# Sums one tick sooner, one gather more in flight, and ScalarE's ticks earlier, in an encoder trunk on one core

## The chip, the cores and the metric

The kernel runs on one core of one Trainium2 chip. The metric is the device time of one execution in microseconds (us). TensorE (PE in the profile), VectorE (DVE), ScalarE (ACT) and GpSimd (POOL) run programs of their own, in order, and wait for one another through semaphores; SyncE (SP) only issues DMA. All DMA queues share the 16 DMA engines of the core.

## What is computed

Two sequences of 256 tokens with 1024 channels go through the same two layers. A layer is

```
x += W_out(sig(gA) * P_A(SSD(n)) + sig(gB) * P_B(DilatedAttn(n))),  n = RMSNorm(x)
x += PEER(RMSNorm(x))
```

SSD is a bidirectional state-space branch in 8 groups, the attention has 24 heads with three dilations, and a last RMSNorm closes the trunk. PEER is the part that the change touches. For each token, 8 heads search two sets of 128 keys, keep the best 16 pairs each, and so choose 128 of 16384 experts. Then

```
hid = gelu(einsum('td,thkd->thk', xb, expert_u[ib]))
out = einsum('thk,thkd->td', gb * hid, expert_v[ib])
```

Each token reads 128 rows of 2048 floats (the u and v halves side by side), all chosen by its own data.

## The kernel before, in words

**Passes.** The work is cut in four passes m (`PASSES`): layer 0 of sequence 0, layer 0 of sequence 1, then layer 1 of each. A pass has a mixer (norm, 8 SSD groups, 4 attention head pairs, 8 merge steps, the output projection, a second norm, 16 query projections, and the routing that yields expert indices and gates) and a PEER part of 256 slots (`SLOTS_P`): two tiles of 128 tokens with 128 slots each. A slot is one expert per token, 128 rows of 8 KB, gathered by one indirect DMA. The PEER part of pass p runs beside the mixer of pass p+1, except its first slots in pass 0 and all 256 of the last pass, which run alone at the end: the tail.

**A slot in steps.** In slot n (k inside its pass):

- POOL gathers the rows into buffer n % NB of eight (`gather`, L559), after the sum of slot n-8 has freed it (`summed`, L461).
- VectorE takes the dot of the u halves with the normed token, into `hid` (L1451).
- ScalarE, once per pair of slots, waits for both dots, computes the gelu (L1041) and two weights (L1046), and for a slot whose sum is on PE a diagonal matrix with the weight (L1054).
- The sum adds weight times v half to the output: on VectorE into x (L1460), or on PE with the diagonal into a PSUM bank (L851). Tables in the code (`BESIDE`, `ON_PE`) say which; in most of the SSD phase odd slots go to PE and even ones to VectorE, in attention and merge nearly all go to VectorE, in the tail all go to PE.

**Ticks.** Each engine has one `tick(p, k)` per slot. VectorE's does the dot of k and then the sum of k - LAG; PE's does the sum of k - LAG (`sums_after`, L155). The last tick of a pass does LAG + 1 sums, and the tick k = 128 + LAG also adds the PE sums of the first tile to x (L1462). ScalarE's acts on odd k. POOL's issues the gather of n + AHEAD, where `AHEAD = NB - LAG - 1`. So 8 buffers hold 4 gathers on their way, one dot, and 3 that wait for their sum.

**The order on each engine** is written out by a planner. `EACH` gives a nominal length in units (about a microsecond each) to every phase, `place(name, i, f)` turns a point in a phase into a position, and the mixers on all engines yield positions between pieces of work. `deal` gives each slot a due position (L105). `together` (L228) runs the ticks due before the next yielded position. ScalarE alone passes a third argument, `BEHIND`: its ticks come that many units later against its mixer work than on the other engines. In the SSD phase a due position comes every 3.6 units, and a group has 42.5.

**Mixer work around the ticks,** as the prediction names it: in SSD group g ScalarE computes 12 decay exponentials twice (L915, for group g-1; the second time just ahead of the second convolution), evacuates four projections with the convolution's middle tap (L943), on which VectorE adds four taps (L1262), then does Silu (L951, L955) and evacuates two small products (L960, L962). VectorE masks the decay rows (L1276), which POOL writes to DRAM (L526) and reads back broadcast (L520) on the queue of the gathers. In the query phase ScalarE evacuates queries (L1024) and key scores (L1018) for VectorE's search (L1096). The projections on PE are L592, with weights loaded by SP into a ring of six units (L488).

Of the kernel before, what the change touches and what calls it, by code (L numbers as in the profile page):

```python
# [66 lines left out]


NB = 8
LAG = 3  # L70
AHEAD = NB - LAG - 1
DIAGS = 5

BEHIND = 3.0


REST = PIECES - PH
# [77 lines left out]
def sums_after(k):  # L155

    return list(range(SLOTS_P - LAG - 1, SLOTS_P)) if k == SLOTS_P - 1 else [k - LAG] if k >= LAG else []

# [69 lines left out]
def together(mixer, tick, late=0.0):  # L228

    for m in range(PASSES):  # L230
        todo = list(PLAN[m])
        for where in mixer(m):
            while todo and todo[0][2] + late <= where:
                tick(*todo.pop(0)[:2])
        while todo:
            tick(*todo.pop(0)[:2])


def build(nc, x_prompt, x_sample, consts, biases, rel, par, w_ssd, w_att, w_mrg, w_out, w_qry, w_uv,
          w_n2, w_final, y_prompt, y_sample):  # L240
    with ExitStack() as ctx:
# [620 lines left out]
        def _(act):  # L862
# [204 lines left out]

            together(mixer, tick, BEHIND)
            for k in range(SLOTS_P):
# [9 lines left out]
        def _(v):  # L1079
# [354 lines left out]
            def add_sums(p, t):  # L1434

                k = SLOTS_T * (t + 1) - 1
                v.wait_ge(v_pe, pe_sums(p, k))
                if dve_sums(p, k):
                    v.wait_ge(v_dve, dve_sums(p, k))
                xo = x[:, 2 * (p % 2) + t, :]  # L1440
                v.tensor_tensor(xo, xo, sum_banks(p, t).rearrange("p b d -> p (b d)"), ALU.add).then_inc(x_add.sem, 1)

            def tick(p, k):
# [8 lines left out]
                for q in sums_after(k):  # L1452
# [5 lines left out]
                    if dve_sums(p, q) > 1:  # L1458
                        v.wait_ge(v_dve, dve_sums(p, q) - 1)
                    v.scalar_tensor_tensor(out=xo, in0=rows[before % NB][:, D:], scalar=wgt[:, q:q + 1], in1=xo,  # L1460
                                           op0=ALU.mult, op1=ALU.add).then_inc(v_dve, 1)
                if k == SLOTS_T + LAG:  # L1462
                    add_sums(p, 0)
# [104 lines left out]
```

## Time and profile before

| | us |
|---|---|
| median of 3 runs | 4060.14 |
| lowest, highest | 4059.96, 4065.61 |
| the profiled execution's own time | 4058.57 |
| span of its profile | 4056.8 |
| PE busy in the span | 3436.7 |
| VectorE busy | 2872.2 |
| ScalarE busy | 1612.8 |
| POOL busy | 1218.2 |
| read from memory | 1439.31 MB |

The profile's page gives busy time by engine, the chain that ended last, groups of instructions, and DMA issues. Busy shares are means over phases with different limits, so the stretches have to be read one by one. In a row of waits the first name is the engine and tile that waited, and the one behind the arrow is what released it. Line numbers are those of the kernel.

### The profile page before, as it was taken

What the parts mean: (1) busy time and instruction counts of PE and PEld (TensorE: products, weight loads), DVE (VectorE), ACT (ScalarE), POOL (GpSimd) and SP (SyncE); (2) the same over time, 40 slices, a digit from 0 to 9 for tenths busy, and PEclk for the clock granted to TensorE, in tenths of its full rate; (3) what the DMA queues carried; (4) which work ended last, traced back from release to release, by engine and by line L of the source; (5) the groups of instructions that cost most, each with busy time, mean ns of one, the idle gap of its engine ahead of it and who ended that gap; (6) DMA issues with size and microseconds to landing.
All of it is one profiled execution on the core that took longest, in us unless ns stands there. A gap on an engine that the chain in (4) does not pass through costs nothing.

```text
span 4056.8 us, 40644 instructions
## 1 busy us (share of the span) xinstructions
PE 3436.7 (85%) x13410; PEld 2350.3 (58%) x13410; DVE 2872.2 (71%) x5740; ACT 1612.8 (40%) x4211; POOL 1218.2 (30%) x1094
## 2 busy tenths in 40 slices
PE   7999997989889787888889787988889886777776
PEld 6877875656667564566667564666667562332222
DVE  3632128898887779899787779899788778655444
ACT  4643013566434223676434223576434222222222
POOL 1000002333333224333333224333333224433332
PEclk9999998989999988999999998999999988999999
DMA  6543447999999988999999989999999979999998
GB/s 205 174 160 127 149 138 293 391 364 396 399 421 423 423 315 353 377 398 412 405 425 420 423 311 355 378 395 415 402 425 419 423 278 365 427 427 427 427 427 351
DMA packets 252119, 1444.49 MB, mean 356 GB/s; under 512 B 31608, under 2 KB 31608, under 8 KB 118788
## 3 DMA queue, kind: packets, MB, share of 16 engines
q0 software_dynamic: 164976, 1133.94, 68.6%
q1 hardware_dynamic: 86800, 307.82, 20.4%
q8 instruction: 107, 1.75, 0.2%
q14 instruction: 104, 0.85, 0.1%
q10 hardware_dynamic: 132, 0.12, 0.0%
HBM read 1439.31 MB, written 7.13 MB: 357 GB/s over the span
## 4 chain that ended last, share of the span: by engine, by line
DMA 30%; PE 28%; DVE 24%; ACT 11%; issue 6%; POOL 1%; DVEq 0%; ACTq 0%; POOLq 0%
DMA rows<-in_w_uv,idx 28%; PE banks L592 16%; DVE rows L1451 7%; DVE x L1460 5%; PE sums L851 4%; ACT arena L915 4%; DVE arena L1262 3%; PE banks L851 2%; PE banks L728 1%; ACT L1041 1%; ACT L915 1%; DMA arena<-a_rows 1%; DVE arena L1288 1%; DVE arena L1359 1%; ACT diag L1054 1%
## 5 line engine op out<-in xcount | busy, mean ns | idle before, releaser
L559 POOL DMA_INDIRECT rows<-in_w_uv,idx x1024 | 1170.8, 1143 | 2209.9 <-DVE x L1460 1309.2
L1451 DVE CUSTOM_DVE_ANT_0 rows<-rows,xn 128x1024 f32<-128x1024 f32 x1024 | 1242.3, 1221 | 521.5 <-DMA rows<-in_w_uv,idx 519.3
L592 PE MATMUL banks<-hT,ring 128*128 128x256 f32 x6656 | 1496.2, 382 | 39.7 <-ACT arena L960 17.3
L592 PEld LDWEIGHTS banks<-hT,ring 128*128 128x128 f32 x6656 | 1267.0, 191 | 293.3 <-issue 92.5
L851 PE MATMUL sums<-rows,diag 128*128 128x512 f32 x1648 | 835.3, 644 | 265.8 <-ACT diag L1054 239.7
L851 PEld LDWEIGHTS sums<-rows,diag 128*128 128x128 f32 x1648 | 322.2, 204 | 656.3 <-ACT diag L1054 325.5
L1041 ACT ACTIVATE gelu<-hid 128x2 f32<-128x2 f32 x512 | 103.7, 203 | 1450.9 <-DVE hid L1451 1449.7
L1460 DVE SCALAR_TENSOR_TENSOR x<-rows,wgt,x 128x1024 f32<-128x1024 f32 x484 | 620.3, 1282 | 31.0 <-ACT wgt L1046 30.0
L1262 DVE SCALAR_TENSOR_TENSOR arena<-banks,pr,arena 128x254 f32<-128x254 f32 (+1 forms) x512 | 245.9, 481 | 119.1 <-ACT arena L943 105.3
L851 PE MATMUL banks<-rows,diag 128*128 128x512 f32 x512 | 239.7, 612 | 76.0 <-ACT diag L1054 76.0
L1046 ACT ACTIVATE wgt<-gelu,gate 128x1 f32<-128x1 f32 x1024 | 246.0, 287 | 16.8
L915 ACT ACTIVATE arena<-arena 128x128 f32<-128x128 f32 x768 | 230.8, 388 | 20.2 <-DVE arena L1276 19.6
L592 PE MATMUL banks<-yT,ring 128*128 128x256 f32 x1024 | 228.4, 380 | 0.7 <-DMA ring<-in_w_mrg 0.6
L851 PEld LDWEIGHTS banks<-rows,diag 128*128 128x128 f32 x512 | 93.3, 192 | 222.4 <-ACT diag L1054 127.9
L592 PEld LDWEIGHTS banks<-yT,ring 128*128 128x128 f32 x1024 | 193.3, 190 | 33.5 <-issue 5.1
L1054 ACT ACTIVATE diag<-cst,wgt 128x128 f32<-128x128 f32 x540 | 193.8, 390 | 4.5
L1041 ACT ACT_TABLE_LOAD x142 | 182.2, 1283 | 2.5
L728 PE MATMUL banks<-ring,hT 128*128 128x384 f32 x512 | 173.3, 492 | 0.0
L1359 DVE CUSTOM_DVE_ANT_1 arena<-banks,arena 128x768 f32<-128x768 f32 x64 | 60.9, 951 | 129.6 <-PE banks L716 129.6
L728 PEld LDWEIGHTS banks<-ring,hT 128*128 128x128 f32 x512 | 95.3, 190 | 71.2 <-issue 12.0
L807 PE MATMUL banks<-ring,arena 128*128 128x512 f32 x256 | 111.8, 595 | 4.8 <-DMA ring<-in_w_out 4.8
L975 ACT ACTIVATE arena<-banks 128x256 f32<-128x256 f32 x96 | 35.9, 380 | 188.5 <-PE banks L592 188.3
(204 smaller groups left out, 2527.9 us busy)
## 6 DMA issues: line engine op xcount, KB each, us to landing
ring<-in_w_ssd SPq DMA_DIRECT2D x192, 512.0 KB, 7.4
ring<-in_w_att SPq DMA_DIRECT2D x144, 512.0 KB, 7.8
ring<-in_w_mrg SPq DMA_DIRECT2D x128, 512.0 KB, 12.4
arena<-a_rows POOLq DMA_DIRECT2D x32, 1024.0 KB, 11.3
ring<-in_w_qry SPq DMA_DIRECT2D x64, 512.0 KB, 5.0
arena<-bias_tiles POOLq DMA_DIRECT2D x16, 1152.0 KB, 9.7
ring<-in_w_out SPq DMA_DIRECT2D x32, 512.0 KB, 17.9
rows<-in_w_uv,idx POOLq DMA_INDIRECT x1024, 12.5
```

What stands on the lines that cost most here:

```text
L559: nc.gpsimd.indirect_dma_start(out=rows[n % NB][:, :], out_offset=None, in_=w_uv, in_offset=bass.IndirectOffsetOnAxis(ap=idx[:, t, s:s + 1 ...
L592: mm = pe.matmul(out, w[:, k * P:(k + 1) * P], rhs[:, k0 + k, :], start=start and k == 0, stop=stop and k == n - 1)
L728: mm = pe.matmul(pb(t, 3 * P), hT[:, k, t * P:(t + 1) * P], w[:, k * 3 * P:(k + 1) * 3 * P], start=(k == 0), stop=(k == KD - 1))
L807: mm = pe.matmul(pb(2 + 2 * t + nh), mT[:, k, t * P:(t + 1) * P], ring_of(u)[:, nh * 512:(nh + 1) * 512], start=k == 0, stop=k == KD - 1)
L851: mm = pe.matmul(sum_banks(p, t)[:, h, :], diag[e % DIAGS][:, :], rows[n % NB][:, D + 512 * h:D + 512 * h + 512], start=q == mine[0], stop ...
L915: ins = act.activation(Eb[:, r, k, :], Eb[:, r, k, :] if src is None else src, ACT.Exp, bias=bneg[:, si, col:col + 1])
L1041: act.activation(gelu[:, k - 1:k + 1], hid[:, k - 1:k + 1], ACT.Gelu).then_inc(g_ge, 1)
L1046: act.activation(wgt[:, q:q + 1], gelu[:, q:q + 1], ACT.Copy, scale=gate[:, t, q % SLOTS_T:q % SLOTS_T + 1]).then_inc(g_w, 1)
L1054: act.activation(diag[e % DIAGS][:, :], ident, ACT.Copy, scale=wgt[:, q:q + 1]).then_inc(d_ok, 1)
L1262: ins = v.scalar_tensor_tensor(out=acc, in0=pb(j)[:, lo + o:lo + o + w], scalar=pr[:, col:col + 1], in1=acc, op0=ALU.mult, op1=ALU.add)
L1451: v.tensor_tensor_reduce(u, u, xn2[:, (n // SLOTS_T) % 3, :], 1.0, 0.0, ALU.mult, ALU.add, hid[:, k:k + 1]).then_inc(u_done, 1)
L1460: v.scalar_tensor_tensor(out=xo, in0=rows[before % NB][:, D:], scalar=wgt[:, q:q + 1], in1=xo, op0=ALU.mult, op1=ALU.add).then_inc(v_dve, 1)
```

## The change

`LAG` goes from 3 to 2, and with it `AHEAD` from 4 to 5; `BEHIND` goes from 3.0 to 1.0. The eight buffers then hold 5 gathers on their way, one dot and 2 that wait for their sum.

```
 NB = 8
-LAG = 3
+LAG = 2
 AHEAD = NB - LAG - 1
 DIAGS = 5
 
-BEHIND = 3.0
+BEHIND = 1.0
```

## Rows read from the trace of the kernel before

**Rows 1.** Stretches: PE, PEld, DVE, ACT, POOL busy (instructions), PE clock, DMA share, GB/s

```profile
740.00:1100.00 360.00, 320.09 (x1303) 227.78 (x1302) 311.79 (x511) 223.33 (x560) 124.24 (x105) 0.95 0.97 388
...
1425.00:1575.00 150.00, 117.34 (x436) 78.84 (x434) 127.34 (x452) 35.05 (x113) 48.65 (x38) 0.89 0.85 319
...
1640.00:2010.00 370.00, 327.75 (x1347) 231.71 (x1346) 323.33 (x528) 229.42 (x576) 132.18 (x113) 0.97 0.98 398
2010.00:2350.00 340.00, 278.74 (x1181) 207.66 (x1180) 268.09 (x384) 116.22 (x277) 115.01 (x102) 0.94 1.01 423
...
3410.00:4056.80 646.80, 485.44 (x1024) 190.01 (x1024) 343.07 (x618) 174.01 (x656) 250.66 (x249) 0.97 0.98 415
```

**Rows 2.** Gathers in 100 us of the tail: POOL busy (gathers), PE clock, DMA share, GB/s

```profile
3500.00:3600.00 100.00, 40.78 (x41) 0.97 1.01 427
```

**Rows 3.** Waits of DVE, 2010 to 2350 and then 3410 to 4056.8: total, times, longest

```profile
DVE rows L1451 <- DMA rows<-in_w_uv,idx: 64.8, 59, 2.5
...
DVE rows L1451 <- DMA rows<-in_w_uv,idx: 288.9, 238, 3.0
```

**Rows 4.** Waits of DVE, 1640 to 2010 (three), then 740 to 1100, 2560 to 2900

```profile
DVE arena L1262 <- ACT arena L943: 15.3, 7, 3.3
DVE rows L1451 <- DMA rows<-in_w_uv,idx: 11.4, 10, 1.7
DVE x L1460 <- ACT wgt L1046: 9.9, 3, 4.5
...
DVE rows L1451 <- DMA rows<-in_w_uv,idx: 5.5, 5, 2.3
...
DVE rows L1451 <- DMA rows<-in_w_uv,idx: 4.0, 4, 2.3
```

**Rows 5.** Waits over the whole span

```profile
ACT gelu L1041 <- DVE hid L1451: 1449.7, 365, 12.9
...
PE sums L851 <- ACT diag L1054: 239.7, 122, 12.9
...
DVE x L1460 <- ACT wgt L1046: 30.0, 10, 4.5
```

**Rows 6.** Groups of the page: busy, mean ns of one, idle before, releaser

```profile
L1460 DVE SCALAR_TENSOR_TENSOR x<-rows,wgt,x 128x1024 f32<-128x1024 f32 x484 | 620.3, 1282 | 31.0 <-ACT wgt L1046 30.0
...
L1046 ACT ACTIVATE wgt<-gelu,gate 128x1 f32<-128x1 f32 x1024 | 246.0, 287 | 16.8
...
L1054 ACT ACTIVATE diag<-cst,wgt 128x128 f32<-128x128 f32 x540 | 193.8, 390 | 4.5
```

**Rows 7.** Timeline, 1774 to 1783: start, us, engine, line, operation, idle before

```profile
1774.65 0.20 ACT L1041 ACTIVATE gelu<-hid 128x2 f32<-128x2 f32 x1
...
1775.71 0.55 ACT L943 ACTIVATE arena<-banks,pr 128x256 f32<-128x256 f32 x1
1776.27 1.28 ACT L915 ACT_TABLE_LOAD   x1
...
1776.29 2.04 DVE L1262 SCALAR_TENSOR_TENSOR arena<-banks,pr,arena 128x254 f32<-128x254 f32 x4 [3.21 <-ACT arena L943]
1777.57 3.62 ACT L915 ACTIVATE arena<-arena 128x128 f32<-128x128 f32 x12
...
1781.73 2.03 DVE L1262 SCALAR_TENSOR_TENSOR arena<-banks,pr,arena 128x254 f32<-128x254 f32 x4
1782.95 0.20 ACT L1041 ACTIVATE gelu<-hid 128x2 f32<-128x2 f32 x1
```

**Rows 8.** Timeline of POOL and then DVE, first SSD group of the pass

```profile
1625.51 0.74 POOL L520 DMA_DIRECT2D arena<-a_rows  x1 [1.31 <-DMA a_rows<-arena]
...
1637.46 2.36 DVE L1276 TENSOR_TENSOR arena<-arena,cst 128x1024 f32<-128x1024 f32 x2 [5.63 <-DMA arena<-a_rows]
```

**Rows 9.** DMA issues of the page: queue, count, KB each, median us to landing

```profile
ring<-in_w_ssd SPq DMA_DIRECT2D x192, 512.0 KB, 7.4
...
arena<-a_rows POOLq DMA_DIRECT2D x32, 1024.0 KB, 11.3
```

**Rows 10.** Timeline of ACT in the query phase

```profile
1490.82 0.38 ACT L1024 ACTIVATE yT<-banks 128x256 f32<-128x256 f32 x1 [2.86 <-PE banks L592]
...
1493.93 0.20 ACT L1041 ACTIVATE gelu<-hid 128x2 f32<-128x2 f32 x1 [2.73 <-DVE hid L1451]
```

## The prediction

> **What bounds the kernel now.** I read the table of stretches first, cut where the phases of a pass change. A pass has three kinds of stretch [rows 1]. In attention and merge (2010 to 2350 us; 1100 to 1425 and 2900 to 3260 read alike) the DMA engines are full, share 1.01 and 423 GB/s, and no other engine is. In the SSD phase (740 to 1100, 1640 to 2010, and 2560 to 2900 alike) the DMA share is 0.97 to 0.98 and VectorE is busy for 323 of 370 us; the queries and the routing (1425 to 1575, twice more after that) leave the DMA at 0.85 with VectorE at 127 of 150 us. The last stretch, 3410 us to the end, is gathers alone at full rate, 41 in 100 us [rows 2]: 2.44 us per gather.
>
> Then the waits of VectorE. Where the DMA is full it waits for gathered rows, 64.8 us in one such stretch and 288.9 us in the last one [rows 3]. In an SSD stretch it waits for ScalarE instead: 15.3 us for a convolution's first tap (L943), 9.9 us for a weight (L1046); rows cost it 11.4 us there, 5.5 and 4.0 us in the two sister stretches [rows 4]. Over the kernel the weight costs VectorE 30.0 us, while ScalarE itself sits 1449.7 us waiting for dots and PE 239.7 us waiting for diagonals [rows 5]. So DMA rate sets some 1670 us, VectorE with ScalarE in its chain most of the rest after the first gather.
>
> **The change, part by part.** AHEAD is NB - LAG - 1, so LAG of 2 alone makes it 5. The gather of slot n+5 stands at POOL's tick n and waits for the sum of n-3, which VectorE or PE now does at tick n-1. The relation of POOL to the sums is the old one; a buffer is given back one tick sooner. No instruction is added or removed, and the order of the sums stays. Moved by one tick are each sum on VectorE and on PE, the addition of a tile's PE sums to x after its first half, and, at the end of a pass, one sum out of the flush (three in place of four), which was on PE and leaves VectorE's flush of three as it is: 0.
>
> *1. Full stretches and the tail.* A fifth gather does not move bytes faster where the share is 1.01 [rows 1]. In the tail POOL, PE and ScalarE have nothing but ticks, each waits for its own slot, and LAG orders nothing: 0. What counts is how far the gathers are ahead when a full stretch begins: VectorE waits for rows all through it [rows 3], so one gather more already in a buffer is one gather less to wait for. That is 2.44 us [rows 2] in each of three passes: -7.3 us. Bounds 0 and -7.3.
>
> *2. Waits for rows in the SSD stretches,* 5.5 + 11.4 + 4.0 = 20.9 us [rows 4], each shorter than one tick. A buffer given back a tick sooner can end any of them, but VectorE may then reach the next wait for ScalarE sooner. Bounds 0 and -20.9; I take a bit over half, -12.
>
> *3. The sum's wait for its weight.* A sum takes 1282 ns, one weight 287 ns and a diagonal 390 ns [rows 6]. An even slot's pair is complete one dot before its sum instead of two; ScalarE needs 0.2 us for the gelu and 0.3 us for the weight, and 1.28 us more for a table if it comes from Exp. With BEHIND 1.0 ScalarE's tick stands two units earlier in its program. Comparing the positions, I find that about 40 of the 128 double ticks of a pass move ahead of a neighbouring item, 17 of them in the SSD phase, and that no table load is added. Three of these move ahead of the decay exponentials (12 ACTIVATEs, 3.62 us). There the weight is early, but the exponentials are late. One case worked out [rows 7]: now the gelu of slots 52 and 53 is at 1774.65, the convolution that VectorE needs is ready at 1776.26, the exponentials start at 1777.57 and the next gelu follows at 1782.95. After the change the sum of slot 52 (1.28 us) goes into VectorE's 3.21 us wait: -1.2. But the tick of slots 54 and 55 moves ahead of the exponentials and holds them until its dot at about 1779.6; 1.1 us of tick, 1.28 of table, 3.62 and 0.55 bring the second L943 to 1786.1, where VectorE starts that convolution at 1781.73 now. In between it can do the sum of slot 54, so +4.4 - 1.3 = +3.1. Nothing moves for the ticks of slots 41 and 67, but their sums come one dot sooner and wait for the same exponentials: some +1.2 and +1.9 by the same working. The two longest weight waits of now (slots 28 and 98) only become waits for exponentials, -0.7 together, and slot 104 adds some 0.9. Net an estimate of +5.4 per pass, +16 in three. Bounds: -30.0, all weight waits gone and nothing in their place [rows 5], and +43: the 15.3 us of L943 [rows 4] nearly doubled in each pass.
>
> *4. POOL's own transfers.* Decay rows go on the queue that the gathers use. In the first SSD group VectorE waits for them: issued at 1625.51, used at 1637.46 after 5.63 us of idle time [rows 8]. They land after 11.3 us where a weight unit on SP's queue takes 7.4 us [rows 9]. One gather more ahead of them is up to 2.44 us [rows 2], unless it fell into idle DMA time before: bounds 0 and +7.3 over three passes, I take +4.5. The Trainium skill, page "DMA: Bandwidth & Descriptors", section "Queues, rings and completion order", says that each DMA engine takes turns between the queue rows that have work, a packet at a time; by that rule the weight loads lose nothing to the fifth gather and the decay rows, in the gathers' row, pay all of it. The sum would then be 3 us higher. The two landing times agree with the rule in direction only.
>
> *5. Queries.* The tick of slot 231 moves ahead of a query evacuation: now the evacuation is at 1490.82 and the gelu at 1493.93 [rows 10]. It holds the evacuation 4.2 us; the key scores that need it are a unit away, so of this about 1 us reaches VectorE: +3 in three passes, bounds 0 and +12.6.
>
> *6. PE.* A sum on PE stands one tick sooner and waits longer for its diagonal. PE runs ahead of VectorE in the SSD phase, so I charge 0: the cover is that lead. If it goes, each pass pays up to 10 us (PE is busy for 328 of 370 us, rows 1, and 35 us more of waits would leave nothing): 0 to +30. The moved ticks also hold Silu of two groups by some 5 us; PE then evacuates its first projection at least 4 us ahead of need, 0.
>
> Sum: -7.3 - 12 + 16 + 4.5 + 3 = +4.2 us on the profiled execution's 4058.57, so 4062.8; that execution is 1.6 us under the median of three, 4060.14. I say 4063. About 0.2%, 8 us, is what a measurement of this kernel can tell from no change.
>
> **Rivals.**
> *A. The early release wins, faster.* If VectorE rarely stands behind the exponentials, item 3 gives back its 30.0 us instead of costing 16, item 2 all 20.9, item 1 its 7.3: 4058.6 - 58 = 4000 at the far end. Half of that, 4030, is likelier, as the L943 waits stay. For it: the long waits of rows 5 are all ScalarE finishing late, and BEHIND of 1.0 goes at that. Against it: what follows those weights is the same ScalarE program. Chance 0.31.
> *B. ScalarE in order holds the mixer, slower.* Place: conv evacuations, exponentials and Silu that stand behind a tick whose dot is late. Each moved item waits for a dot that VectorE does only after its own mixer work. Price: +43 instead of +16 in item 3, and 12.6 in item 5: about +41 on the forecast's terms, 4100. It decides once the waits for L943 pass some 25 us per SSD stretch. For it: ScalarE already idles 1449.7 us for dots. Against it: VectorE's use of a convolution is three units behind ScalarE's place, so much of a delay is covered. Chance, with a smaller version at 4075: 0.25.
> *C. PE loses its lead.* Item 6 at 30: 4092. It decides where the diagonal waits of PE in an SSD stretch grow past the 40 us it has idle. Chance 0.09.
> **How the numbers follow.** Forecast case (terms cancel, 4052 to 4072) 0.35, A 0.31, B 0.25, C 0.09. The forecast case lies within 8 us of the median for nearly all its weight; a little of it, 0.02, is slower. So faster 0.31, same 0.33, slower 0.36. The forecast's own range is 4048 to 4078; for 8 in 10 it reaches to the middle of A, 4032, and into B and C, 4094.
>
> **What would show it.** In the changed profile: the span of the last stretch (first tail dot to the end) unchanged within 2 us; DMA share in the full stretches still 1.01; the wait for rows in SSD stretches under 10 us in all; the gelu soon after its dot before exponentials, but more wait for L943 or for the sums' weights, some 30 us per pass together against 25 now; the wait for decay rows 1 to 2.5 us longer per pass; PE's diagonal waits up without L592 work arriving late. If the weight waits fall to near nothing and L943 stays at 15 us, A is right; if L943 or the decay exponentials rise past 25 us per stretch, B is. A tail that changes, or full stretches that lose share, would prove the reading of the bound wrong.

## The result and the profile after

The changed kernel is slower: 4110.46 us (median of 4 runs, 4106.84 to 4114.64) against 4060.05 us before on the same chip, a ratio of 1.0123 with a 95% interval of 1.011 to 1.0136. The forecast was 4063 us with a range up to 4094 us. The span of its profile is 4112.8 us against 4056.8; the profiled execution, 4114.64 us, is the slowest of the four.

The first view is the table of stretches of the kernel after, cut at the same events of VectorE in each pass: first convolution of the SSD phase, first scores of attention, first addition of the output projection, first dot of the next pass. Columns as in [rows 1]. The first row is pass 1's SSD phase, the second its stretch with full DMA (attention to output); then come pass 2's norm, SSD phase, full stretch and queries, and last the tail.

```profile
710.00:1079.00 369.00, 325.05 (x1279) 227.23 (x1278) 307.07 (x534) 220.24 (x551) 122.92 (x106) 0.94 0.95 370
1079.00:1431.00 352.00, 318.48 (x1380) 235.60 (x1379) 274.54 (x401) 126.92 (x300) 121.73 (x105) 0.97 1.01 418
...
1587.00:1624.00 37.00, 22.12 (x80) 14.40 (x81) 24.62 (x46) 17.36 (x37) 9.78 (x9) 0.73 0.85 330
1624.00:2001.00 377.00, 330.31 (x1288) 230.08 (x1287) 314.22 (x544) 222.24 (x558) 128.99 (x110) 0.93 0.97 374
2001.00:2370.00 369.00, 325.36 (x1380) 241.02 (x1378) 289.24 (x420) 128.96 (x309) 130.12 (x111) 0.95 1.01 416
2370.00:2526.00 156.00, 117.60 (x436) 78.42 (x436) 134.94 (x462) 40.03 (x121) 49.20 (x41) 0.87 0.86 331
...
3464.00:4112.80 648.80, 479.94 (x1024) 187.68 (x1024) 344.65 (x621) 174.00 (x656) 249.80 (x252) 0.98 0.98 415
```

The kernel before, cut at the same events, has this for pass 2 and the tail:

```profile
1575.00:1605.00 30.00, 21.85 (x95) 16.43 (x96) 23.33 (x45) 16.47 (x33) 9.08 (x9) 0.83 0.95 376
1605.00:1960.00 355.00, 315.74 (x1273) 222.26 (x1272) 313.39 (x545) 222.57 (x561) 127.42 (x110) 0.97 0.98 396
1960.00:2332.00 372.00, 319.65 (x1379) 237.05 (x1377) 289.66 (x420) 129.81 (x309) 127.17 (x112) 0.96 1.01 419
2332.00:2490.00 158.00, 116.77 (x436) 78.81 (x436) 135.44 (x463) 40.18 (x120) 52.24 (x41) 0.90 0.84 319
...
3408.00:4056.80 648.80, 485.44 (x1024) 190.01 (x1024) 344.57 (x620) 174.01 (x656) 252.10 (x251) 0.97 0.98 415
```

VectorE is busy for the same time in the SSD phase, 313 and 314 us, but the phase takes 377 us and not 355. With the starts of these events to a tenth, over all passes:

| us | before | after | difference |
|---|---|---|---|
| norm, three passes | 68.8, 30.1, 30.0 | 72.1, 37.3, 37.3 | +17.8 |
| SSD | 354.4, 354.6, 354.3 | 368.5, 376.4, 376.3 | +57.9 |
| attention to output | 355.4, 372.1, 371.7 | 352.2, 369.1, 368.5 | -9.4 |
| queries and routing | 158.7, 158.2, 161.8 | 155.9, 155.8, 156.3 | -10.7 |
| tail, first dot to last addition | 638.1 | 637.8 | -0.3 |

These make +55.3, and the start adds 0.8, of the spans' 56.0. So the DMA-bound stretches and the tail came out near the forecast; the SSD phase alone cost more than the whole loss.

The granted clock of TensorE moved, too: in the three SSD stretches from 0.95, 0.97 and 0.96 to 0.94, 0.93 and 0.94, and PE was busy 9 to 15 us longer in each. No run holds the clock apart from the waits.

The second view is the waits of VectorE in the SSD phase of pass 2 of the kernel after, 1624 to 2001 us. Its first two rows answer to [rows 4]:

```profile
DVE x L1460 <- ACT wgt L1046: 29.4, 10, 6.7
DVE arena L1262 <- ACT arena L943: 18.9, 8, 4.2
DVE arena L1276 <- DMA arena<-a_rows: 5.3, 1, 5.3
...
```

The wait for weights went from 9.9 to 29.4 us (in pass 1 from 10.2 to 24.3, in pass 3 from 9.9 to 29.4): +53.1 us where the three phases grew by 57.9. The waits for L943 grew less, from 23.4, 15.3 and 14.6 us to 25.1, 18.9 and 19.1. The wait for rows is gone from the list. Over the whole span, to be held against [rows 5]:

```profile
ACT gelu L1041 <- DVE hid L1451: 1514.1, 379, 13.4
...
PE sums L851 <- ACT diag L1054: 386.1, 146, 20.6
...
DVE arena L1262 <- ACT arena L943: 112.5, 45, 4.7
DVE x L1460 <- ACT wgt L1046: 95.5, 39, 6.7
```

The third view shows one such wait in the timeline of the kernel after, ScalarE and VectorE:

```profile
1839.06 3.61 ACT L915 ACTIVATE arena<-arena 128x128 f32<-128x128 f32 x12
...
1839.99 1.22 DVE L1451 CUSTOM_DVE_ANT_0 rows<-rows,xn 128x1024 f32<-128x1024 f32 x1
1841.13 0.08 DVE L1451 DVE_READ_ACCUMULATOR2_ANT hid<- 128x1 f32 x1
1842.69 1.28 ACT L1041 ACT_TABLE_LOAD   x1
1843.99 0.20 ACT L1041 ACTIVATE gelu<-hid 128x2 f32<-128x2 f32 x1
1844.22 0.48 ACT L1046 ACTIVATE wgt<-gelu,gate 128x1 f32<-128x1 f32 x2
1844.55 1.28 DVE L1460 SCALAR_TENSOR_TENSOR x<-rows,wgt,x 128x1024 f32<-128x1024 f32 x1 [3.34 <-ACT wgt L1046]
```

The late weight is that of slot 64 of its pass, counted in the order of the sums. The pair's second dot ended at 1840.0, while ScalarE was in the exponentials. VectorE had one more dot to do, to 1841.2, and then stood 3.34 us: until the exponentials ended at 1842.7, the table load and the gelu ran, and the first weight was there. Counted in the same way, all 39 weight waits of the kernel after, and all 10 of the kernel before, stand at even slots.

### The profile page after: what moved, and what is told of

It reads as the page before. It is cut to its first block, busy times and chain, and to the rows that moved or that the text cites. A ratio compares the mean times of both kernels' runs of the same rounds, so it can differ in the third digit from the quotient of the medians.

```text
span 4112.8 us, 40646 instructions
## 1 busy us (share of the span) xinstructions
PE 3461.5 (84%) x13410; PEld 2353.6 (57%) x13410; DVE 2872.4 (70%) x5740; ACT 1610.6 (39%) x4211; POOL 1222.4 (30%) x1094
## 4 chain that ended last, share of the span: by engine, by line
PE 32%; DMA 24%; DVE 23%; ACT 14%; issue 6%; POOL 1%; DVEq 0%; ACTq 0%; POOLq 0%
DMA rows<-in_w_uv,idx 23%; PE banks L592 19%; DVE rows L1451 7%; PE sums L851 5%; DVE x L1460 4%; ACT arena L915 4%; DVE arena L1262 3%; ACT L1041 2%; PE banks L851 1%; PE banks L728 1%; ACT L915 1%; DVE arena L1288 1%; PE banks L766 1%; ACT diag L1054 1%; ACT wgt L1046 1%
## 5 line engine op out<-in xcount | busy, mean ns | idle before, releaser
L851 PE MATMUL sums<-rows,diag 128*128 128x512 f32 x1648 | 855.7, 656 | 393.4 <-ACT diag L1054 386.1
L1460 DVE SCALAR_TENSOR_TENSOR x<-rows,wgt,x 128x1024 f32<-128x1024 f32 x484 | 620.2, 1281 | 96.5 <-ACT wgt L1046 95.5
## 6 DMA issues: line engine op xcount, KB each, us to landing
ring<-in_w_mrg SPq DMA_DIRECT2D x128, 512.0 KB, 11.6
arena<-a_rows POOLq DMA_DIRECT2D x32, 1024.0 KB, 10.1
```

What stands on the lines that cost most here:

```text
L851: mm = pe.matmul(sum_banks(p, t)[:, h, :], diag[e % DIAGS][:, :], rows[n % NB][:, D + 512 * h:D + 512 * h + 512], start=q == mine[0], stop ...
```

## The experiments

The kernel before took 4060 to 4063 us (medians) beside these runs; each ratio is to the kernel before measured beside that run.

**BEHIND alone.** Everything as before, ScalarE's ticks earlier.

```
 LAG = 3
-BEHIND = 3.0
+BEHIND = 1.0
```

> LAG 3 and AHEAD 4 as before, BEHIND 1.0 as after. Theory W (VectorE's even sums wait for weights because only one dot is left as cover): no such waits return, so the time is that of before or a little less, 4045 to 4065 us, and L1460's wait for the weight falls from 30 us to under 20. Rival M (ScalarE's reordered program holds the mixer): it keeps most of the loss, 4090 to 4110 us.

4079.48 us, ratio 1.0039 (1.0024 to 1.0053). Between the two theories: ScalarE's order costs some 16 us of its own. The weights are no longer waited for (2.0 us over the whole span), and the convolutions are. Over the span of this run:

```profile
PE sums L851 <- ACT diag L1054: 219.1, 117, 12.9
...
DVE arena L1262 <- ACT arena L943: 135.8, 53, 5.0
```

L943's wait rose from 105.3 to 135.8 us. What the earlier weight gave, 30.0 us, the later convolution took. The SSD phases sum to 1066.0 us against 1063.3, so most of the 16 us is outside them: in attention to output (+9.4), the queries (+4.5) and the norms (+2.4).

**The lag of one engine at a time.** VectorE and PE get a lag each; AHEAD stays at 5 and BEHIND at 1.0.

```
-LAG = 2
-AHEAD = NB - LAG - 1
+LAG = 3
+PE_LAG = 2
+AHEAD = 5
...
-def sums_after(k):
+def sums_after(k, lag):
...
-                for q in sums_after(k):
+                for q in sums_after(k, PE_LAG):
...
-                if k == SLOTS_T + LAG:
+                if k == SLOTS_T + max(LAG, PE_LAG):
```

> The changed kernel, but VectorE's sums three ticks behind again; PE's stay at two, BEHIND at 1.0, AHEAD at 5. Theory W: nearly all of the 50 us comes back, 4055 to 4070 us, with VectorE's wait for weights under 30 us. Rival P (PE, held for diagonals, loses its lead): 4095 to 4115 us, with PE's wait for diagonals still near 386 us.

4091.14 us, ratio 1.007 (1.0053 to 1.0087). Neither theory alone: 12 us more than with BEHIND alone, so PE's shorter lag costs something, but it is not the main part. Against BEHIND alone the SSD phases grew by 21.3 us, and ScalarE's wait for PE's projections (L943) over the span from 27.3 to 53.7 us; attention and the queries gave 11.6 back.

The mirror image has `LAG = 2` (VectorE) and `PE_LAG = 3`.

> The changed kernel, but PE's sums three ticks behind again; VectorE's stay at two. Theory W: the loss stays, 4095 to 4115 us, with VectorE's wait for weights near 95 us. Rival P: 4055 to 4070 us, with PE's wait for diagonals near 240 us.

4106.19 us, ratio 1.0114 (1.0097 to 1.0131): 27 us more than with BEHIND alone, 43 us of cost in the SSD phases less what other stretches gave back. The clock in the SSD stretches was 0.94 in this run, too, but ScalarE waited no longer for PE's projections than before (27.1 us against 36.3), so the clock did not reach VectorE by that way. The waits of the two runs, first VectorE three and PE two ticks behind (its lines are one further down the file):

```profile
PE sums L852 <- ACT diag L1055: 386.9, 154, 21.1
DVE arena L1263 <- ACT arena L944: 142.9, 56, 5.7
...
```

and then VectorE two and PE three:

```profile
PE sums L852 <- ACT diag L1055: 228.9, 114, 12.9
DVE arena L1263 <- ACT arena L944: 111.5, 44, 4.6
DVE x L1461 <- ACT wgt L1047: 91.1, 36, 6.7
```

Each engine's lag moves its own wait and leaves the other's: the weight wait (91.1 of after's 95.5 us) belongs to VectorE's lag, the diagonal wait (386.9 of 386.1) to PE's. The three steps, 16 for BEHIND, 27 for VectorE and 12 for PE, add to 55 us where the change cost 50. They do not simply add: with VectorE at two ticks already, the change's own 4110 us (ratio 1.0123) is only some 4 us above this run (1.0114), less than the intervals can tell from nothing.

**The gather's place.** The changed kernel with POOL's gathers one tick later in its program.

```
-AHEAD = NB - LAG - 1
+AHEAD = 4
```

> The changed kernel with AHEAD at 4: POOL's gathers one tick later in its program against its mixer work. Theories W and P: no change against after, 4105 to 4115 us, because a gather's buffer is freed by the same sum. Rival G (the gather that stands ahead of POOL's own transfers delays them): 5 to 15 us less than after.

4114.64 us, ratio 1.0131 (1.0114 to 1.0148): no difference from after. So the place of the gathers against POOL's own transfers costs nothing that shows. Most gathers of both kernels wait for the sum that frees their buffer (POOL's waits of this kind are 2077 us after and 1917 us here); that these sums alone set how many gathers are on their way is a reading of that, not a run.

**Which slots VectorE sums.** VectorE two ticks behind, PE three, and in groups 2 to 7 of the SSD phase (the only row of the table with 50 per cent) odd slots on VectorE instead of even ones.

```
-             (i + 1) * percent // 100 > i * percent // 100)
+             (i + 1 + (percent == 50)) * percent // 100 > (i + (percent == 50)) * percent // 100)
```

> VectorE's sums two ticks behind, PE's three, as in the run with 4106 us; in the SSD phase the odd slots' sums are now on VectorE and the even ones' on PE, so each sum has at least two dots between its pair's last dot and itself. Theory W (one dot is too little cover for an even slot on VectorE): the waits for weights fall from 91 us to under 35 us and the time to 4070 to 4085 us. Rival R (what costs is that every sum of VectorE comes sooner in its program, whatever its slot): 4100 to 4110 us.

4066.23 us, ratio 1.0016 (1.0007 to 1.0026): 40 us less than with even slots, all of the VectorE part and more. The weight wait fell from 91.1 to

```profile
DVE x L1461 <- ACT wgt L1047: 33.1, 15, 5.4
```

Of the 15 waits that are left, 13 stand at even slots. The number of sums on each engine, the lag, the buffers and the gathers are as in the run with 4106 us. Only the slots changed: an odd slot's pair is complete two dots before its sum, an even slot's one.

The same slots in the full change (PE two ticks behind, too):

> The changed kernel with the odd slots' sums on VectorE in the SSD phase, so that the even ones' sums, with one dot of cover, are on PE. Theory W with PE as a second, smaller cost: waits for weights under 40 us, PE's waits for diagonals 400 us and over, 4075 to 4090 us. Rival Q (one dot of cover costs as much on PE as on VectorE): 4100 us and over.

4088.47 us, ratio 1.0067 (1.0052 to 1.0083). It is 22 us under after, and 22 us over the run with PE at three. PE's waits for diagonals are 404.3 us; one dot of cover costs on PE, too, but about half of what it costs on VectorE. ScalarE then waits for projections:

```profile
ACT arena L943 <- PE banks L592: 85.9, 30, 5.4
```

In after that wait is 51.0 us, before it was 36.3.

And in the kernel before, whose lag is three:

> The kernel before (LAG 3, BEHIND 3.0) with the odd slots' sums on VectorE in the SSD phase. Theory W: an odd slot has one dot more between its pair and its sum than an even one, so the 30 us of waits for weights fall to under 8 us; what is behind them is again ScalarE, so 0 to 15 us faster, 4045 to 4060 us. Rival R (the slot does not matter): waits of 30 us stay, no change.

4064.25 us, ratio 1.0006 (0.9997 to 1.0015): no change. The weight waits fell only to 24.2 us from 30.0, and PE's for diagonals rose to 292.0 from 239.7. With two dots of cover already there, the slot hardly matters.

**The table loads.** Exp in place of Gelu on the pair of dots, in the kernel after and in the kernel before. The expert weights are then exp and not gelu of the dots, so what flows into the next layer, and the rows that it gathers, are others as well.

```
-                act.activation(gelu[:, k - 1:k + 1], hid[:, k - 1:k + 1], ACT.Gelu).then_inc(g_ge, 1)
+                act.activation(gelu[:, k - 1:k + 1], hid[:, k - 1:k + 1], ACT.Exp).then_inc(g_ge, 1)
```

> The changed kernel with Exp in place of Gelu on the pair of dots, so that most table loads beside the decay exponentials go; the output is not the reference's. Theory T (the loads of 1.28 us are a large part of a late weight): the waits for weights fall to about half, 40 to 60 us, and the loss against the same edit of before to 15 to 35 us. Rival X (the 12 exponentials of 3.62 us alone): waits of 75 us and over, loss still about 45 us.

> The kernel before with Exp in place of Gelu; the output is not the reference's. It is the base of the other run with this edit. Theory T: 20 to 40 us faster than before, 4025 to 4045 us, since VectorE's waits for L943 and weights shrink; rival X: within 10 us of before.

4032.07 us and 4015.96 us, ratios 0.9933 (0.9917 to 0.995) and 0.9899 (0.9882 to 0.9915). The table loads in front of the pair fell from 142 to 73 in both, and those in front of the exponentials from 53 to 8. The same change now costs 16 us, not 50, and VectorE waits for weights and convolutions like this after:

```profile
DVE arena L1262 <- ACT arena L943: 79.1, 40, 4.6
...
DVE x L1460 <- ACT wgt L1046: 35.0, 27, 3.9
```

Theory T holds, and by more than its ranges (4016 us is below its 4025, and 35.0 us below its 40): with the same exponentials, 60 of the 95 us of weight waits were the loads' part. One dot of 1.2 us covers 0.5 us of gelu and weight, but not 1.28 us of load ahead of them.

**How far behind.** The changed kernel, `BEHIND = 2.0`.

> The changed kernel with BEHIND at 2.0. If ScalarE's earlier ticks help at a lag of two (theory H): weights come later again and the time rises, 4115 to 4130 us. If they hurt at this lag as they do at three (theory M): waits for L943 fall from 112 us, and the time falls by 5 to 15 us, 4095 to 4105 us.

4111.54 us, ratio 1.0131 (1.0114 to 1.0148): as at 1.0, and neither theory's time. The waits for weights rose to 107.7 us from 95.5, those for L943 stayed (112.8), and the norm got 2.5 us shorter in one pass. LAG 2 cannot run with BEHIND 3.0: in that order of the programs the engines wait for one another in a circle. So what BEHIND alone cost, 16 us, is measured at a lag of three only.

The best placement of sums (VectorE two with odd slots, PE three), `BEHIND = 2.5`:

> The run of 4066 us (VectorE two ticks behind with odd slots, PE three) with BEHIND at 2.5. Theory M (early ticks of ScalarE hold L943): waits for L943 fall from 127 us to 105 to 115, weights wait a little more, 4045 to 4062 us: the best of lag and order, at or below before. Rival: BEHIND has no effect at this lag, 4062 to 4070 us.

4042.75 us, ratio 0.996 (0.9947 to 0.9974): faster than both kernels. In pass 2's SSD phase, 1601 to 1952 us, VectorE waits

```profile
DVE x L1461 <- ACT wgt L1047: 14.3, 4, 5.7
DVE arena L1263 <- ACT arena L944: 13.4, 7, 2.8
```

Three more runs took it apart. Even slots on VectorE in it:

> The best version so far (4043 us: VectorE two ticks behind, PE three, odd slots on VectorE, BEHIND 2.5), but with the even slots on VectorE again. Theory W: as at BEHIND 1.0, the even slots cost some 40 us: 4075 to 4100 us, waits for weights over 90 us. Rival B (BEHIND 2.5 made the gain): 4040 to 4055 us.

4092.94 us, ratio 1.008 (1.0063 to 1.0096), 50 us more. Over the whole span the waits are these, where the run with odd slots has 61.1 us for weights and 94.6 us for L944:

```profile
DVE x L1461 <- ACT wgt L1047: 133.4, 54, 7.0
DVE arena L1263 <- ACT arena L944: 78.6, 32, 5.7
```

The slot carries the effect here as at 1.0. With VectorE three ticks behind in it:

> The best version so far, but with VectorE three ticks behind too (and four gathers on their way). Theory G (the buffer that comes free a tick sooner is worth something once no sum waits more for it): 4055 to 4070 us. Rival B (BEHIND 2.5 made the gain): 4040 to 4050 us.

4051.04 us, ratio 0.9975 (0.9965 to 0.9985). It lies between the two ranges that I had, and the intervals of the two runs touch: the shorter lag may be worth some 6 us by the ratios once no sum pays for it, but that is not shown. And the kernel before with `BEHIND = 2.5` alone:

> The kernel before with BEHIND at 2.5 and nothing else. Between 3.0 (4060 us) and 1.0 (4079 us) at this lag. Theory M (earlier ticks of ScalarE cost in proportion): 4060 to 4070 us. Rival B: 4040 to 4052 us.

4049.03 us, ratio 0.9974 (0.9964 to 0.9984). I had it at 4060 to 4070 or at 4040 to 4052; it is the second. BEHIND does not act in proportion: 4060 at 3.0, 4049 at 2.5, 4079 at 1.0. The waits for L943 over the span hardly changed (104.6 us against 105.3), but those for weights fell from 30.0 to 15.7 us, and the SSD phases from 1063.3 to 1049.9 us, which is all of the gain. Why 2.5 keeps both waits low, where 1.0 trades one for the other, was not taken apart. The run with 4043 us, which has the shorter lag and the other slots as well, is 6 us below this one, and their intervals touch.

## Why the prediction was wrong, by its own steps

**What bounds the kernel** was right: the DMA in three stretches and the tail, VectorE with ScalarE in its chain in the SSD phase.

**Item 1** came out right in size. The full stretches became 3.2, 3.0 and 3.2 us shorter; the forecast was one gather of 2.44 us each, and the tail unchanged. Together -9.4 for -7.3 forecast. Part of this is luck: BEHIND alone made these stretches 9.4 us longer, which item 1 has no term for, so the shorter lags gave some 19. That one gather more in a buffer is what gave it was not tested.

**Item 2**, the rows VectorE waits for in the SSD phase, happened and brought nothing. The waits are gone from the list, but the time that I credited, -12 us, did not come: the stretches grew. There was also less to gain than the 20.9 us that I read. My windows ran 26 to 50 us into attention; cut at the events, the SSD phases had 0.8, 3.4 and 4.6 us of such waits.

**Item 3 is the step that failed.** It put the weights and what they displace at +5.4 us per pass, +16 in all, with +43 as the bound. Measured, VectorE's lag costs 27 us and BEHIND 16 us. The two waits that I put at some 30 us per pass together are 48 to 49. The mechanism stood in it: an even slot has one dot of cover, a table load and the exponentials come before its weight. The size was wrong in two ways. I followed seven slots of one pass, picked from the old timeline, and added their costs; after the change VectorE waited for 10 weights in that phase and for 39 in all. In order they are slots 18, 38, 40, 52, 64, 66, 76, 84, 96 and 100, and only the pairs of 40, 52 and 66 were among mine. The case that I worked out shows it best. The sum of slot 52 did move ahead of the convolution, but its weight stood behind the first exponentials and a table load, so in place of the 1.2 us that I credited it waited 3.36:

```profile
1794.66 3.61 ACT L915 ACTIVATE arena<-arena 128x128 f32<-128x128 f32 x12
1798.29 1.28 ACT L1041 ACT_TABLE_LOAD   x1
...
1800.15 1.28 DVE L1460 SCALAR_TENSOR_TENSOR x<-rows,wgt,x 128x1024 f32<-128x1024 f32 x1 [3.36 <-ACT wgt L1046]
```

The other slots looked safe in the old timeline, whose order the change itself was moving; that this is why they were missed is a reading of the timelines, not a run. The second error: I let the two longest waits of before turn into waits for exponentials at no cost, where with two dots of cover, at BEHIND 1.0, weights are hardly waited for at all and the convolutions cost 30 us more. The upper bound took L943's wait as what would grow, when the weight's did.

**Item 4** charged 4.5 us for decay rows that land later. The wait for them in passes 2 and 3 is 5.3 and 5.0 us against 5.6 and 5.0 before, their median time to landing is 10.1 us against 11.3, and a place one tick later for the gather changes nothing. It was 0. The rule that it cited (the Trainium skill, page "DMA: Bandwidth & Descriptors", section "Queues, rings and completion order": turns between the queue rows) would have had the decay rows pay for the whole gather ahead of them; no run here shows that they do, and these landing times speak against it.

**Item 5** charged +3 for the queries, which became 10.7 us shorter. BEHIND alone made them 4.5 us longer, in the item's direction; the shorter lags, which it left out, more than undid that. The tick of slot 231 was read right in the timeline, but the whole was not: sums on PE come sooner there, and VectorE's waits for key scores fell (20.2 us before, 15.6 us after in the queries of pass 1).

**Item 6** charged nothing for PE. PE's shorter lag costs 12 us while VectorE's is three, 22 us with VectorE at two and odd slots, and in the change itself, with even slots, some 4 us that are not clear of noise. The cost does not come where the item looked for it: PE's waits for diagonals in an SSD stretch stay at 29 to 31 us, under the 40 that it has idle, but ScalarE waits longer for PE's projections (53.7 us against 27.3 in the run with PE alone at two). At a few points PE's lead is gone altogether. The clearest is the norm of pass 2. The prediction had no term for the norms, which grew by 17.8 us in all. Here is PE's timeline after, with the sum ahead of the transposes (L604) that the next projection needs:

```profile
1594.32 3.75 PE L851 MATMUL sums<-rows,diag 128*128 128x512 f32 x4 [9.30 <-ACT diag L1054]
1597.87 3.15 PE L604 MATMUL banks<-cst,arena 128*128 128x128 f32 x16
```

The dots for this sum stand behind the norm on VectorE (the normed tile is written from 1590.44 to 1591.9), so PE cannot transpose until they, the gelu and the diagonal are done, 6 us after the tile was ready. Before, the sums stood behind the transposes:

```profile
1579.20 3.65 PE L604 MATMUL banks<-cst,arena 128*128 128x128 f32 x16 [6.32 <-DVE arena L1210]
1586.80 5.23 PE L851 MATMUL sums<-rows,diag 128*128 128x512 f32 x8 [3.95 <-DVE hT L1216]
```

Counted from the pass's first dot (1587.0 and 1574.9 us) the transposes start after 10.9 us in place of 4.3: 6.5 of the 7.2 us that the norm grew in this pass. With PE alone at two ticks it took 32.1 us, with VectorE alone 32.4, and not 37.3: it takes both.

**The rivals.** A, the early release, was wrong, although two of its parts (rows, one gather ahead) showed. B, ScalarE in order, forecast 4100 us and came nearest in time, but by luck: its place was only a third of the loss, and L943's wait went to 25.1, 18.9 and 19.1 us in the three SSD stretches, just at its own decision point of 25 in one and under it in two. C, PE's lead, was there with 4 to 12 us of the 30 allowed, and by another way than it named. All three costs came together, where the forecast took them as alternatives; that, with item 3, is why the range ended 16 us short.

## What to carry to other kernels

Before shortening a software pipeline by a tick, count for each kind of item how much of the consuming engine's own work is left between its producer and its use, and put the producer's worst neighbour in front of it (here 3.62 us of exponentials and a 1.28 us table load against one dot of 1.2 us). Where items are made in pairs, the first of the pair has the least cover: give it to the engine that can wait, and the shorter lag is affordable (4066 us in place of 4106). Shifting the pairing might do the same; it was not tried. When an order is balanced against another parameter, vary that one alone in small steps first; here a half unit of it was worth 11 us, more than the shorter lag brought in any run.

## What was not expected of the hardware

Nothing in the chip itself: a table load took 1.28 us in every group, and the tail took 637.8 to 639.1 us in every kernel. What surprised was how little of the time table loads explain by their own length: with Exp in place of Gelu the loads fell from 312 (400.3 us) to 172 (220.9 us), so 179 us went from ScalarE in the kernel before, and 44 us from its time (4060 to 4016), though ScalarE is idle for more than half of the span.
